# Mixture-of-experts loop in one transformer kernel: tokens of two experts in one gather, gate and up weights in three places, result pieces in another order

## What is computed

```python
def expert_block(args):
    xb, e = args
    return (jax.nn.silu(xb @ w_gate[e]) * (xb @ w_up[e])) @ w_down[e]

y_buf = lax.map(expert_block, (x_buf, blk_e)).reshape(n_slots, d)
out = jax.ops.segment_sum(y_buf.astype(f32) * w_buf[:, None], tok_buf, num_segments=n_tok + 1)
...
x = x + g2 * moe_x.reshape(b, n_tok, d)
...
return rms_norm_2(x, norm_final)
```

## Time and profile before

| | us |
|---|---|
| median of 3 runs | 1509.04 |
| lowest and highest | 1508.01, 1509.62 |
| span of the profiled execution | 1505.5 |
| PE, DVE, ACT, POOL busy in it | 1441.6, 891.3, 541.5, 102.8 |

### The profile page before, as it was taken

How to read it: one execution, slowest core, us unless ns; L and a number is a source line. 1 busy time by engine, 2 the same in 40 slices (tenths; PEclk the granted TensorE clock), 3 DMA queues, 4 the chain that set the end, 5 groups by cost and what they waited for, 6 DMA issues and landing times.

```text
span 1505.5 us, 20726 instructions
## 1 busy us (share of the span) xinstructions
PE 1441.6 (96%) x7928; PEld 993.9 (66%) x7928; DVE 891.3 (59%) x1608; ACT 541.5 (36%) x990; POOL 102.8 (7%) x134
## 2 busy tenths in 40 slices
PE   9999999999999999999998998989999999999996
PEld 7886667888888888887887777764434443444333
DVE  4856884567787667774665785553434444444435
ACT  5555774443453432252436885411111111111102
POOL 0001000000000000001003330010101010100100
PEclk9999999999999999999999999999999999999998
DMA  8213010345544357723111105468999999999994
GB/s 262 94 56 127 2 57 21 109 152 148 146 127 120 105 195 265 254 70 110 31 57 71 53 19 215 168 261 351 414 403 410 405 409 399 410 398 400 407 414 192
DMA packets 113739, 312.59 MB, mean 208 GB/s; under 512 B 14143, under 2 KB 65759, under 8 KB 92139
## 3 DMA queue, kind: packets, MB, share of 16 engines
q1 hardware_dynamic: 110131, 303.30, 54.3%
q0 software_dynamic: 3200, 7.87, 1.6%
q10 hardware_dynamic: 312, 0.10, 0.0%
HBM read 311.18 MB, written 4.25 MB: 210 GB/s over the span
## 4 chain that ended last, share of the span: by engine, by line
PE 83%; DVE 5%; DMA 4%; ACT 4%; issue 2%; SPq 2%; POOL 0%; DVEq 0%; POOLq 0%; ACTq 0%
PE bank L1527 75%; PE bank L1530 8%; DMA arena<-in_w_up 4%; SPq L945 1%; DVE hTc L2713 1%; ACT hT_high L1181 0%; ACT arena L1441 0%; SPq L942 0%; ACT ring L1410 0%; DVE hT L2724 0%; DVE ring L2512 0%; DVE weights_low L2130 0%; DMA xn<-normed_tokens,token_index 0%; DVE arena L2561 0%; ACT weights_high L1110 0%
## 5 line engine op out<-in xcount | busy, mean ns | idle before, releaser
L1527 PE MATMUL bank<-weights_high,hT_high 128*128 128x512 f32 (+2 forms) x672 | 234.3, 383 | 5.7 <-DVE hT_low L2176 3.8
L1527 PE MATMUL bank<-weights_low,hT_high 128*128 128x512 f32 (+2 forms) x528 | 198.9, 377 | 0.0
L2130 DVE TENSOR_TENSOR weights_low<-ring,weights_high 128x2048 fp32r<-128x2048 f32 (+2 forms) x59 | 131.0, 2221 | 107.7 <-ACT weights_high L1110 106.9
L1527 PE MATMUL bank<-hT_high,weights_high 128*128 128x512 f32 (+1 forms) x448 | 170.0, 379 | 1.5 <-DVE hT_low L2176 1.5
L1527 PE MATMUL bank<-hT_high,weights_low 128*128 128x512 f32 (+1 forms) x448 | 167.6, 374 | 0.0
L1527 PE MATMUL bank<-hT_low,weights_high 128*128 128x512 f32 (+1 forms) x448 | 167.6, 374 | 0.0
L1110 ACT ACTIVATE weights_high<-ring 128x2048 fp32r<-128x2048 f32 (+2 forms) x59 | 109.5, 1855 | 156.5 <-PE bank L1527 146.7
L1527 PEld LDWEIGHTS bank<-weights_high,hT_high 128*128 128x128 f32 x672 | 126.3, 188 | 29.8 <-issue 6.7
L2713 DVE TENSOR_TENSOR hTc<-bank,mod_gain 128x512 f32<-128x512 f32 x32 | 22.1, 691 | 187.9 <-PE bank L1530 187.9
L1527 PE MATMUL bank<-ring,hTc 128*64 128x512 f32 (+1 forms) x544 | 120.8, 583 | 0.0
L1527 PEld LDWEIGHTS bank<-weights_low,hT_high 128*128 128x128 f32 x528 | 99.3, 188 | 17.8 <-issue 0.2
(11 more groups left out here) (356 smaller groups left out, 2444.2 us busy)
## 6 DMA issues: line engine op xcount, KB each, us to landing
arena<-in_w_down SPq DMA_DIRECT2D x16, 2048.0 KB, 15.7
ring<-in_w_gate SPq DMA_DIRECT2D x32, 1024.0 KB, 12.9
ring<-in_w_up SPq DMA_DIRECT2D x32, 1024.0 KB, 15.1
ring<-in_w_down SPq DMA_DIRECT2D x16, 2048.0 KB, 16.1
arena<-in_w_gate SPq DMA_DIRECT2D x30, 1024.0 KB, 14.1
arena<-in_w_up SPq DMA_DIRECT2D x30, 1024.0 KB, 16.1
xn<-in_w_ada SPq DMA_DIRECT2D x48, 512.0 KB, 4.6
ring<-in_w_up SPq DMA_DIRECT2D x44, 512.0 KB, 5.2
```

Of the source, the lines that this page charges most:

```text
L1527: return nc.tensor.matmul(o, lhsT, rhs, start=start, stop=stop)
L2130: low_ready.tick(v.tensor_tensor(part_view(w_low, key), raw_view(key), part_view(w_high, key), ALU.subtract), k)
```

## The change

- **Gather and transposes**: `gather` brings the 64 rows of two experts as 128 rows, once every two turns, into one buffer `xg`. The indices come from two copies of 64 rows instead of one of 128. PE makes eight transposes of 128 rows a pair: four (`half` 0) in the even turn and four (`half` 1) in the odd turn before the pair is used, all through bank 0. The first pair is transposed ahead of the loop through banks 0 and 3. DVE scales each half with four `tensor_scalar` operations on 128 columns. `xT` has two places, one a pair.
- **Gate and up weights**: the place of expert 2 becomes a third one that is used again and again (`GATE_UP`, `WAYS` = 3). Gate and up of expert `n + 3` are asked for in turn `n`, down of expert `n + 2` as before. SP's loop is written out. The final gain is loaded after all the weights.
- **Pieces**: in an odd turn one piece stands ahead of gate and up and one behind the transposes of the hidden values (`pieces_ahead`, `pieces_behind`). Even turns stay as they were.

The diff, cut to its core:

```diff
-        xg = carve(0, 2, D, of=spare)
-        xT, gu = packed([(2, KT, BLK), (2, 512)], of=hTc_flat, limit=2048)
+        xg = carve(0, D, of=spare)
+        xT_even, gu = packed([(KT, P), (2, 512)], of=hTc_flat, limit=2048)
+        xT = [xT_even, carve(D, KT, P, of=spare)]
...
+        GATE_UP = [EXPERT_SLOTS[0:2], EXPERT_SLOTS[3:5], [early_gate, early_up[:, :]]]
+        DOWN = [EXPERT_SLOTS[2], EXPERT_SLOTS[5]]
+        WAYS = len(GATE_UP)
...
+        def pieces_ahead(n):
+
+            return pieces_of_turn(n)[:n % 2]
+
+        def pieces_behind(n):
+
+            return pieces_of_turn(n)[n % 2:]
...
-            for half, landed in enumerate((first_in, second_in)):
-                sp.wait_ge(landed[1], 16)
-                load_rows(sp, 2, 0, 1, half, early_up[:, :])
+            for half in range(2):
+                load_rows(sp, 2, 2, 1, half)
...
-            for landed in first_in[0:2] + second_in[0:2]:
-                sp.wait_ge(landed, 32)
-            load_gate_and_up(sp, 4, 0, 1)
-            load_down(sp, 2, 0, 1)
-            load_expert(sp, 3, 1, 2)
-            sp.wait_ge(gu_filled, 3)
+            for half in range(2):
+                load_rows(sp, 2, 2, 0, half)
+            for n in range(E - 2):
+                if n + WAYS < E:
+                    load_gate_and_up(sp, n + WAYS, n % WAYS, n + 1)
+                load_down(sp, n + 2, n % 2, n + 1)
+            sp.wait_ge(gu_filled, E - 2)
             sp.dma_start(final_gain, inp["norm_final_2"].partition_broadcast(P)).then_inc(final_in, 16)
-            load_down(sp, 4, 0, 3)
-            load_expert(sp, 5, 1, 4)
-            with sp.Fori(3, E // 2) as it:
-                for par in range(2):
-                    load_expert(sp, 2 * it + par, par, 2 * it + par - 1)
...
+                g.tensor_copy(tok_at[0:BLK, at:at + 1], tok_of[0:BLK, bass.ds(first, 1)]).then_inc(index_ready, 1)
+                g.tensor_copy(tok_at[BLK:P, at:at + 1], tok_of[BLK:P, bass.ds(second, 1)]).then_inc(index_ready, 1)
+                after = held(pool, 2 * n + 2)
                 pool.wait_ge(const_in, CONST_ALL)
                 pool.wait_ge(index_ready, after)
-                g.indirect_dma_start(xg[0:BLK, par, :], None, h_d, bass.IndirectOffsetOnAxis(
-                    ap=tok_at[0:BLK, par:par + 1], axis=0), bounds_check=T - 1, oob_is_err=False).then_inc(
-                        tokens_in[par], 16)
-
-            for n in range(E):
-                gather(n, n, n % 2, n - 1 if n >= 2 else None)
+                g.indirect_dma_start(xg, None, h_d, bass.IndirectOffsetOnAxis(
+                    ap=tok_at[:, at:at + 1], axis=0), bounds_check=T - 1, oob_is_err=False).then_inc(tokens_in, 16)
+
+            for m in range(E // 2):
+                gather(m, 2 * m, 2 * m + 1, 2 * m if m else None)
...
-            def tokens_in_place(n, par, kpar):
-
-                loads, before = held(pe, 16 * kpar + 16), held(pe, n) if not isinstance(n, int) or n else None
-                pe.wait_ge(const_in, CONST_ALL)
-                pe.wait_ge(tokens_in[par], loads)
-                if before is not None:
-                    pe.wait_ge(xt_scaled, before)
-                for j in range(KT):
-                    last = tr(ps[0][:, j * BLK:(j + 1) * BLK],
-                              xg[0:BLK, par, :].rearrange("p (q j) -> p j q", j=KT)[:, j, :], BLK)
+            def tokens_in_place(m, half, bank, read):
+
+                if half == 0:
+                    pe.wait_ge(const_in, CONST_ALL)
+                    pe.wait_ge(tokens_in, held(pe, 16 * m + 16))
+                if read is not None:
+                    pe.wait_ge(xt_ready, held(pe, read))
+                for j in range(KT // 2):
+                    last = tr(bank[:, j * P:(j + 1) * P],
+                              xg.rearrange("p (q j) -> p j q", j=KT)[:, half * (KT // 2) + j, :])
                 last.then_inc(xt_filled, 1)
...
-            tokens_in_place(0, 0, 0)
+            for half, bank in enumerate((ps[0], ps[3])):
+                tokens_in_place(0, half, bank, None)
             unread(ps[1], 7)
             route_act.wait(pe, "rows")
             for n in range(E):
-                if n % 2 == 1:
-                    for pair, t in pieces_of_turn(n):
-                        pair_piece(pair, t)
-                gate_and_up(n, n % 2, n // 2, (early_gate, early_up[:, :]) if n == 2 else None)
-                if n + 1 < E:
-                    tokens_in_place(n + 1, (n + 1) % 2, (n + 1) // 2)
+                for pair, t in pieces_ahead(n):
+                    pair_piece(pair, t)
+                gate_and_up(n // 2, n % 2, n % WAYS, n // WAYS)
+                if n + 2 < E:
+                    tokens_in_place(n // 2 + 1, n % 2, ps[0], n + 2)
                 hidden_transposed(n, n % 2)
...
-                if n % 2 == 0:
-                    for pair, t in pieces_of_turn(n):
-                        pair_piece(pair, t)
+                for pair, t in pieces_behind(n):
+                    pair_piece(pair, t)
...
+            def tokens_scaled(step, half, bank, into):
+
+                dve.wait_ge(xt_filled, step + 1)
+                for j in range(KT // 2):
+                    at = half * (KT // 2) + j
+                    last = v.tensor_scalar(into[:, at, :], bank[:, j * P:(j + 1) * P], mod_gain[:, 2, at:at + 1],
+                                           mod[:, 0, 3, at:at + 1], ALU.mult, ALU.add)
+                last.then_inc(xt_ready, 1)
```

More of the change, by code:

```diff
@@ L849, in rope, with load_rows @@
             return last
-        def load_rows(sp, e, par, i, half, gate=None):
+        def load_rows(sp, e, place, i, half):
             name = ("w_gate_2", "w_up_2")[i]
@@ L855, in load_rows @@
             at = slice(half * 4 * EF, (half + 1) * 4 * EF)
-            into = EXPERT_SLOTS[3 * par + i] if gate is None else gate
-            sp.dma_start(into[:, at], rows[:, at]).then_inc((first_in, second_in)[half][2 * par + i], 16)
+            sp.dma_start(GATE_UP[place][i][:, at], rows[:, at]).then_inc((first_in, second_in)[half][2 * place + i], 16)
         def load_down(sp, e, par, reuse):
@@ L871, in load_gate_and_up @@
                 for i in range(2):
-                    load_rows(sp, e, par, i, half)
-        def load_expert(sp, e, par, reuse):
-            load_gate_and_up(sp, e, par, reuse)
-            load_down(sp, e, par, reuse)
+                    load_rows(sp, e, place, i, half)
         def modulation(sp, parts):
@@ L958, in _ @@
             squared.wait(sp, ("mix2", TT - 1, 0))
-            load_expert(sp, 0, 0, None)
+            load_gate_and_up(sp, 0, 0, None)
+            load_down(sp, 0, 0, None)
             banks.filled(sp, ("out2", TT - 1, 1))
-            load_expert(sp, 1, 1, None)
+            load_gate_and_up(sp, 1, 1, None)
+            load_down(sp, 1, 1, None)
             normed.wait(sp, ("norm2_2", TT - 1, 0))
@@ L1085, in _ @@
                     g.tensor_copy(late[:, 1:2], place_weight[:, bass.ds(i + E, 1)]).then_inc(late_ready, 1)
-                    gather(i + E, i + E, 0, i + E)
+                    gather(i + E // 2, i + E, i + E, held(pool, 2 * i + E))
             pool.wait_ge(final_in, 16)
@@ L2094, in _ @@
                 with pe.Fori(0, later_n) as i:
-                    tokens_in_place(i + E, 0, i + E // 2)
-                    gate_and_up(i + E, 0, i + E // 2)
+                    for half in range(2):
+                        tokens_in_place(i + E // 2, half, ps[0], 2 * i + (E + half))
+                    gate_and_up(i + E // 2, 0, 0, i + -(-E // WAYS))
                     hidden_transposed(i + E, 0)
@@ L2750, in result @@
                 v.tensor_tensor(y_low[:, place, :], y_scaled, y_high[:, place, :], ALU.subtract).then_inc(y_low_ready, 1)
-            tokens_scaled(0, 0, None)
+            for half, bank in enumerate((ps[0], ps[3])):
+                tokens_scaled(half, half, bank, xT[0])
             route_act.wait(dve, "rows")
             for n in range(E):
-                if n % 2 == 1:
-                    for pair, t in pieces_of_turn(n):
-                        added(t, pair * TT + t + 1)
-                if n + 1 < E:
-                    tokens_scaled(n + 1, (n + 1) % 2, n if n >= 1 else None)
+                for pair, t in pieces_ahead(n):
+                    added(t, pair * TT + t + 1)
+                if n + 2 < E:
+                    tokens_scaled(n + 2, n % 2, ps[0], xT[(n // 2 + 1) % 2])
                 hidden_done(n, n % 2, n - 1 if n >= 2 else None)
-                if n % 2 == 0:
-                    for pair, t in pieces_of_turn(n):
-                        added(t, pair * TT + t + 1)
+                for pair, t in pieces_behind(n):
+                    added(t, pair * TT + t + 1)
                 if n == E - 1:
@@ L2769, in _ @@
                 with dve.Fori(0, later_n) as i:
-                    tokens_scaled(i + E, 0, i + E)
+                    for half in range(2):
```

(1 more changed line is left out.)

48 lines of the change are left out of this document (18 added, 30 removed).

## The result

| | before | after |
|---|---|---|
| median, us | 1508.53 (4 runs) | 1493.86 (4 runs) |
| lowest and highest | 1507.84, 1509.62 | 1492.78, 1495.09 |
| span of the profiled execution | 1505.5 | 1493.3 |

The changed kernel is faster: 0.9898 of the time before, 95% interval 0.9887 to 0.991, some 14.7 us. The forecast was 1511.4 us and its range began at 1505. The time is outside it.

What follows compares the result with a forecast made beforehand. DMA was taken to bind the loop, 15.8 us a turn: hole -5.1, final gain -1.3, later turn 0 +1.8, then PE's 14.1 us after down 30, so down 31 begins 2.4 us later: 1511.4 us, range 1505 to 1518.

Steps and rivals of the forecast that it cites:

- the two open costs: PE's clock after its last wait, 0 to 1.7 us, and a gather's DMA cost beyond its bytes; nothing taken for either.
- what a gather costs the DMA engines beyond its bytes: DMA in the loop: 0.6 us a gather, taken to hang on rows, so no change; on gathers, up to 9 us saved.
- Gathers are the cost, rows are not: Rival, DMA in the loop: fewer gathers save 3 to 9 us, about 1505 us, 1502.4 at best; chance 14%.
- The reading of the gathers' fixed time as latency: DMA gathers: the skill's 2.0 us fixed time is latency only; as occupation, fifteen fewer would save some 30 us.
- Steps 1 to 3: DMA queue: down 31 landed at 1484.5; filling the hole at 1040 gives -5.1 us, final gain behind weights -1.3 us.
- Step 4: Start of the kernel: turn 0 and all loads later by 1.8 us, bounds 0.6 to 3.5, through the larger first gather.
- Step 5: End of the DMA queue: down 31 lands at 1479.9, down 30 directly ahead of it 5.2 us earlier, at 1474.7.
- Step 6: End of PE's loop: down 31 begins 14.1 us after PE's wait for down 30, at 1488.9, 2.4 us later than before.
- PE's turn: PE in the loop: about 14.3 us a turn, 1.5 less than DMA's 15.8, so its gain doesn't reach the end.
- The clock: PE after its last wait: a fall to the lower clock may cost 0 to 1.7 us; nothing taken.
- The gather comes late: Rival, loop: gather landing from 14.6 us on makes PE wait, at most 31 us; 0.7 us late gives 1519; chance 10%.
- the marks set for being wrong: Loop rate above 412 GB/s between 1070 and 1470, PE waiting for the gather, or down 30 not PE's last wait.

Runs made afterwards that it cites:

- the control: Changed kernel with two gate-and-up places and old load order, plus one unread 128-row gather a pair from the third pair on: 1501.33 us, ratio 0.9956.
- the two-gather run: Changed kernel with each pair's tokens fetched by two gathers of 64 rows instead of one of 128: 1510.78 us, ratio 1.0012.
- the run with the downs first: Changed kernel, from turn 16 on asking for down n + 2 ahead of gate and up n + 3: 1484.96 us, ratio 0.9842.
- the second run: Kernel before, its 32 gathers in the 128-row form with the upper 64 indices out of bounds: 1510.0 us, ratio 1.0003.

## Why the prediction was wrong

- **The step that failed is one of the two open costs**, "what a gather costs the DMA engines beyond its bytes". The gap was read rightly, (422 - 406)/422 x 400 us, 15.2 us. It was put down to rows, "as I take it", so that nothing changed, with 9 us at the most if it hung on gathers. It hung on neither. With the same rows in gathers of the 128-row form it is gone (422 GB/s with 16 gathers, 421 with 30 in the control) or mostly gone (416 with 32 whose upper half is empty), and with 64-row gathers it is back in full (404). By the two-gather run this is worth some 16 us, where the sum had nothing. The rival *Gathers are the cost, rows are not* pointed the right way, at 14%, with the wrong cause and too small a bound.
- **The bound of that cost had no ground.** "Up to 15 x 0.6" assumed that a 128-row gather costs at least what a 64-row one does. No row of before showed a gather of 128 rows, and the sum had a gain of 15.2 us, the whole gap, as its far end: 1511.4 - 15.2 = 1496.2. The reading of the gathers' fixed time as latency held: 14 gathers more cost 10.1 us in the control, 8.7 of them by their bytes. But it says nothing of the form, which was the question.
- **Steps 1 to 3** (down 31, the hole, the final gain): the hole is filled at 419 GB/s and the gain behind the weights. But filling it is worth nothing that the runs show: with the hole back and down 30 ahead of gate and up 31 the time was 1491.27 us, with the hole filled and the same order 1491.17.
- **Step 4** (turn 0 later, +1.8): SP's first load came at 1010.96 instead of 1008.25, +2.7, inside the bounds of 0.6 to 3.5, but mostly by luck. The first gather itself was issued 2.4 us later in that execution (998.56, not 996.16), of which the second index copy explains 0.24. In the profiles of the other kernels with the new gather it was issued anywhere from 994.77 to 998.57, so a single profile can't show a term of this size. From the gather's issue to SP's first load were 12.4 us, against 12.1 before. PE waited 1.93 us for the gather where it was 1.14, and eight transposes took 1.28 us, not 1.5. After that wait the clock fell, and turn 0 with it came later: the seven products took 3.19 us at a granted clock of 0.50, which the sum didn't have.
- **Step 5** (down 30 lands at 1474.7): it landed at 1459.96, 14.7 us earlier. This is the failed step's price, and the whole error of the span (1507.9 forecast, 1493.3 measured). The error of the median is 17.5 us; the other 2.9 come from adding a difference of spans to the median, which lay 3.5 us above the profiled span before and lies 0.6 above it after.
- **Step 6** (PE's 14.1 us from down 30 to down 31) held: PE went on at 1460.02, and down 31 followed the transposes of 1472.52 and one piece, at about 1474.3, 14.3 us. Behind it 19.0 us to the end of the span, as before. That the order of the last two down loads costs something also held: the runs that put downs ahead gained 2.7 and 8.9 us.
- **PE's turn** (14.3 us) held: where PE doesn't wait two turns take 28.3 us (1065.09 to 1093.35 in the run with the downs first). DVE's four operations take 1.37 us, not 1.0, and still end in time under the piece. "So this gain doesn't reach the end" was right only because DMA was taken to stay at 15.8 us a turn. With DMA at 15.2 PE's old turns would have ended last, as the second run shows. The gain needed both, though the new transposes and scaling were enough on PE's side, as the run with the old pieces and places shows.
- **The clock** (0 taken): PEclk is 1.00 over the loop after, 0.97 before. It fell once, behind the longest wait (3.23 us, from 1304.61): it is 0.61 from 1307.8 to 1312, and 56 records took 13.42 us where they take 11.82 elsewhere. PE waited for the transfers again two turns later, so this lay under them. After waits of up to 2.1 us in the loop it did not fall.
- **The gather comes late**: it did not. Its median from issue to landing is 10.1 us, under the 11 to 14 forecast, and PE waits for it in the loop nowhere. (The 1519 us given for this rival is 10 us on the time before; on the forecast it would be 1521.)

The rest of the picture came as told: PE's waits for down weights from about 1200 us on, down 30 as the last of them, loads of 25 us. Of the marks set for being wrong the rate above 412 GB/s came, and it is the one that points at the failed step.

## What to carry to other kernels

Where transfers run at full share but at 4% less than their best rate, look at what runs beside them: gathers of 64 rows that begin at partition 0 (2% of the bytes) cost the large ones 15 us here. Give such a transfer 128 partitions, or let it begin at partition 32. Two limits within a per cent of each other hide each other's gains: a part of a change that gives nothing alone may carry it with another part. In a loop that waits for weights, the last loads' order counts by the work that stands behind each.

## What the runs showed that was not expected

- Down loads cut into two halves of 64 partitions brought the whole queue to 225 GB/s in the profiled run, and a turn to some 28 us. If only those halves ran at half rate, a turn would take 15.2 + 5.0 = 20.2 us. Why transfers into 128 partitions suffer as much stays open.
- 32 gathers in the 128-row form with the upper half empty gave 416 GB/s, not 422. The number isn't the reason: the control has nearly as many in the same window (24, not 25) and runs at 421. An explanation, not tested, is that the rows then load half of the DMA engines only.
- The part of the kernel ahead of the loop, the same in all runs with the new gather, reached its first gather at 994.77 to 998.57 us. Times read inside two profiles have to be counted from a common point such as turn 0 before they are compared. The medians of several runs carry this spread too, so differences of 1 or 2 us between them aren't told apart here.
